# Both choices of three tiles summed on GpSimd, two tiles weighted there and scaled on ScalarE, in both tails of a two-layer hybrid step

## The reference

```python
def _rmsnorm(x, g):
    y = xf * rsqrt(mean(xf * xf, -1) + RMS_EPS) * g

for l in range(2):
    h = _rmsnorm(x, w['norm_mix'][l])
    mix = ...                      # l = 0: pool + mLSTM; l = 1: S5 + GLU
    x = x + mix
    x = x + _hmoe(_rmsnorm(x, w['norm_ffn'][l]), ...)   # each token: two experts, weighted
return _rmsnorm(x, w['norm_final']), states...
```

## Time and profile before

| what | us |
|---|---|
| median of 3 runs | 1101.48 (1100.95 to 1108.13) |
| span of the profiled execution | 1102.2 |
| TensorE busy | 951.2 (86%) |
| VectorE busy | 424.4 (39%) |
| GpSimd busy | 345.8 (31%) |
| ScalarE busy | 182.6 (17%) |

### The profile page before, as it was taken

One profiled execution on the slowest core, in us unless ns is written; L12 is line 12 of the kernel. 1 busy time (PEld: TensorE's weight loads), 2 busy tenths in 40 slices (PEclk: granted clock), 3 DMA queues, 4 the chain that ended last, 5 costly groups with the idle time before them and its releaser, 6 DMA issues.

```text
span 1102.2 us, 15831 instructions
## 1 busy us (share of the span) xinstructions
PE 951.2 (86%) x5716; PEld 576.6 (52%) x5716; DVE 424.4 (39%) x945; ACT 182.6 (17%) x353; POOL 345.8 (31%) x613
## 2 busy tenths in 40 slices
PE   3999989899888878787887379999989999787786
PEld 2788878555554444444445256444455555344442
DVE  5301155756652223223237971113465323221226
ACT  5311020222210000000034322102351000000003
POOL 1278900282266766656641000000020121101100
PEclk9999999899898999999998789999978999999998
DMA  7126850650679999999991964804046999999964
GB/s 255 39 77 225 302 236 3 251 181 33 266 282 391 425 419 421 408 405 409 401 346 69 102 83 171 363 5 168 19 165 274 419 421 425 424 423 424 424 271 189
DMA packets 53600, 292.39 MB, mean 265 GB/s; under 512 B 11633, under 2 KB 22001, under 8 KB 34071
## 3 DMA queue, kind: packets, MB, share of 16 engines
q1 hardware_dynamic: 41607, 270.29, 63.1%
q0 software_dynamic: 8640, 16.03, 3.9%
q10 hardware_dynamic: 3296, 5.31, 1.8%
HBM read 270.47 MB, written 36.80 MB: 279 GB/s over the span
## 4 chain that ended last, share of the span: by engine, by line
PE 54%; DMA 28%; DVE 6%; SPq 5%; issue 3%; POOL 2%; ACT 1%; POOLq 0%; DVEq 0%; ACTq 0%
DMA arena<-in_w_gu 16%; PE ps L734 13%; PE ps L858 10%; PE ps L1002 9%; PE ps L1197 5%; DMA arena<-in_w_down 4%; PE ps L992 3%; DMA arena<-scratch_hd,idx_now 2%; SPq L565 2%; DMA arena<-scratch_yd 2%; PE ps L929 2%; PE ps L1154 2%; DMA arena<-scratch_kp 2%; PE ps L1150 2%; PE ps L888 2%
## 5 line engine op out<-in xcount | busy, mean ns | idle before, releaser
L1002 PE MATMUL ps<-arena 128*64 128x256 f32 x2048 | 238.9, 389 | 52.6 <-DMA arena<-in_w_gu 52.6
L1002 PEld LDWEIGHTS ps<-arena 128*64 128x64 f32 x2048 | 148.4, 140 | 143.5 <-DMA arena<-in_w_gu 45.9
L2345 POOL TENSOR_TENSOR arena<-arena 128x256 f32<-128x256 f32 (+3 forms) x192 | 132.3, 689 | 41.7 <-POOL arena L2345 41.4
L734 PE MATMUL ps<-arena 128*128 128x260 f32 x640 | 141.7, 383 | 0.0
L2246 POOL TENSOR_TENSOR arena<-arena 128x32 f32<-128x32 f32 (+5 forms) x202 | 93.0, 461 | 155.1 <-DMA arena<-in_s_d 74.1
L992 PE MATMUL ps<-arena 128*64 128x512 f32 x512 | 125.1, 632 | 13.9 <-DMA arena<-in_w_down 13.3
L734 PEld LDWEIGHTS ps<-arena 128*128 128x128 f32 x640 | 121.1, 190 | 18.7 <-issue 0.4
L858 PE MATMUL ps<-arena 128*128 128x512 f32 x256 | 118.7, 616 | 3.9 <-DVE arena L1758 3.7
L1977 DVE TENSOR_TENSOR arena<-arena,ps 128x128 f32<-128x128 f32 x64 | 18.3, 288 | 255.7 <-ACT arena L1447 255.6
L1447 ACT ACTIVATE arena<-ps 128x128 f32<-128x128 f32 x64 | 17.7, 277 | 467.9 <-PE ps L1002 467.9
L1593 DVE TENSOR_TENSOR arena<-arena 128x32 f32<-128x32 f32 (+18 forms) x125 | 70.2, 561 | 36.1 <-DMA arena<-scratch_rows 22.2
(11 more groups left out here) (225 smaller groups left out, 971.6 us busy)
## 6 DMA issues: line engine op xcount, KB each, us to landing
arena<-in_w_gu SPq DMA_DIRECT2D x64, 2048.0 KB, 13.1
arena<-in_w_down SPq DMA_DIRECT2D x64, 1024.0 KB, 13.9
arena<-in_w_in SPq DMA_DIRECT2D x10, 1024.0 KB, 6.0
scratch_yd<-arena SPq DMA_DIRECT2D x2, 4160.0 KB, 18.7
arena<-scratch_yd SPq DMA_DIRECT2D x16, 512.0 KB, 7.9
arena<-in_w_out SPq DMA_DIRECT2D x1, 4096.0 KB, 12.1
scratch_hd<-arena ACTq DMA_DIRECT2D x8, 512.0 KB
arena<-in_w_glu SPq DMA_DIRECT2D x2, 2048.0 KB, 7.7
```

The lines of the kernel that those rows point to most:

```text
L734: mm = pe.matmul(o[:, b, 0:HALF], w[:, kc, (n % 2) * P:(n % 2 + 1) * P], HT[:, kc, b * HALF:(b + 1) * HALF], start=kc == 0, stop=kc == KC - 1)
L1002: mm = pe.matmul(ps[CAP * f:CAP * f + CAP, 2 + s, 0:256], XT[l][:, kc, CAP * s:CAP * s + CAP], WGU[l][i][s][:, kc, 256 * f:256 * f + 256], ...
L2345: g_.tensor_tensor(o, x, y, f).then_inc(sem("matrix_steps"), 1)
```

## The change

In both tails:

- GpSimd adds both choices of the last three tiles in order (k = 2, 3, 4) into the first one's place (`summed`). TensorE's `stored(k)` is dropped for these; its sum in PSUM is the last pair's rows alone. VectorE's `add_stored(k)` for k of 2 and more now waits for that sum (`choices_summed`) as well.
- GpSimd multiplies X of k = 0 and 1 by the norm's vector (`weighted`, into `WEIGHTED`), and ScalarE scales these rows by the reciprocal root (`scaled_rows`), k = 0 behind `tile_root(2)` and k = 1 behind the last root. VectorE scales only k = 2, 3, 4. In layer 0 ScalarE's first one also waits for `rows_added`, which VectorE gives after the last stored add and `add_last(3)`.
- VectorE's order is rewritten around that.
- Waits for `h_2` and `h_4` become waits for three tiles and for ScalarE's two; SP's final stores go in the order of tiles 0, 2, 3, 1, sample rows.
- The final norm's vector has a place of its own, `GBF`, and its load is issued between the waits for the two scatter counters, ahead of all loads of gathered rows.
- The semaphores of the first input loads and of the gathered rows are one family now (`tile_in_i`), with counts to match.

```diff
+        GBF = place(A + 21504, D)
+        WEIGHTED = [[place(A + at, D) for at in (8192, 9216)], [YG[1][t][1] for t in range(2)]]
...
                 sp.wait_ge(sem(f"y_out_{l}_1"), 112)
+                if l:
+                    load(GBF, T["norms"][4], "norm_in")
                 sp.wait_ge(sem(f"y_out_{l}_0"), 128)
-                for k, t in enumerate(combined_order(l)):
+                for t in combined_order(l):
                     for j in range(2):
                         at = NT * j + P * t
-                        load(YG[l][t][j][0:ROWS[t]], yd[l][at:at + ROWS[t]], f"yg_in_{t}")
-                    if l and k == 0:
-                        load(GB, T["norms"][4], "norm_in")
+                        load(YG[l][t][j][0:ROWS[t]], yd[l][at:at + ROWS[t]], f"tile_in_{t}")
...
-            for i in range(TILES):
-                sp.wait_ge(sem("h_4"), i + 1)
+            for i, (ready, n) in ((0, ("rows_by_act", 3)), (2, ("h_4", 1)), (3, ("h_4", 2)), (1, ("rows_by_act", 4))):
+                sp.wait_ge(sem(ready), n)
...
                         picked(0)
+                        stored(1)
                         for k in range(1, 5):
                             if k == 3 and l == 0:
                                 pe.wait_ge(sem("m_copied"), 17)
                             if k == 4:
                                 pe.wait_ge(sem(f"combined_{l}"), 1)
-                            stored(k)
                             picked(k)
...
+                def scaled_rows(k):
+
+                    t = combined_order(l)[k]
+                    act.wait_ge(sem("weighted_by_pool"), 2 * l + k + 1)
+                    act.wait_ge(sem("rstd_ready"), 2 * l + k + 1)
+                    if l == 0:
+                        act.wait_ge(sem("rows_added"), 1)
+                    out, src = norm_of_experts(l, t)[1], WEIGHTED[l][k]
+                    a.activation(out, src if l else by_group(src), ACT.Copy, scale=rstd[:, t:t + 1]
+                                 ).then_inc(sem("rows_by_act"), 1)
+
                 for k, t in enumerate(combined_order(l)):
                     act.wait_ge(sem(f"combined_{l}"), k + 1)
                     tile_squares(act, 2 * l + 2, t, JUNK[l], k)
                     tile_root(act, 2 * l + 2, t, k)
+                    if k == 2:
+                        scaled_rows(0)
+                scaled_rows(1)
                 if l == 0:
-                    act.wait_ge(sem("h_2"), 4)
+                    act.wait_ge(sem("h_2"), 2)
                     fill_pad(step)
...
-                        for k in range(3):
-                            add_stored(k)
+                        add_stored(0)
+                        add_stored(1)
                         add_last(0)
-                        add_stored(3)
+                        add_stored(2)
+                        variance(0)
                         add_last(1)
-                        variance(0)
-                        add_stored(4)
+                        for k in range(2):
+                            add_stored(k + 3)
+                            recip(k)
+                            dve.sem_inc(sem("rstd_ready"), 1)
+                            variance(k + 1)
+                            add_last(k + 2)
+                        dve.sem_inc(sem("rows_added"), 1)
+                        variance(3)
                         dve.wait_ge(sem("norm_in"), 8 * nn_ + 16)
-                        for k in range(5):
-                            if k < 3:
-                                add_last(k + 2)
-                            if k < 4:
-                                variance(k + 1)
+                        recip(2)
+                        add_last(4)
+                        scale(2)
+                        variance(4)
+                        for k in (3, 4):
+                            recip(k)
                             scale(k)
...
+                        def summed(k):
+                            t = order[k]
+                            m = ROWS[t]
+                            pool.wait_ge(sem(f"tile_in_{t}"), 32 * l + 48)
+                            one, other = (YG[l][t][j][0:m] for j in range(2))
+                            g_.tensor_tensor(one, one, other, ALU.add).then_inc(sem("choices_summed"), 1)
+
+                        def weighted(k):
+                            t = order[k]
+                            pool.wait_ge(sem("norm_in"), 16 * l + 32)
+                            pool.wait_ge(sem(f"combined_{l}"), k + 1)
+                            pool.wait_ge(sem(f"down_done_{l}"), E)
+                            g_.tensor_tensor(WEIGHTED[l][k], X[:, t, :], GBF if l else GB, ALU.mult
+                                             ).then_inc(sem("weighted_by_pool"), 1)
+
+                        summed(2)
+                        weighted(0)
+                        summed(3)
+                        summed(4)
+                        weighted(1)
```

More of the change, by code:

```diff
@@ L434, in norm_of_experts @@
             if l:
-                return X[:, t, :], HC[:, t, :], GB
+                return X[:, t, :], HC[:, t, :], GBF
             if t == TILES:
@@ L482, in _ @@
             for i in range(TILES):
[L483 removed]
+                load(X[:, i, :], every_fourth(T["x_prompt"], i), f"tile_in_{i}")
                 if i == 0:
@@ L587, in turns @@
                         sp.wait_ge(sem(f"combined_{l}"), r + 4)
-                        sp.wait_ge(sem(f"h_{2 * l + 2}"), 5)
+                        sp.wait_ge(sem(f"h_{2 * l + 2}"), 3)
+                        sp.wait_ge(sem("rows_by_act"), 2 * l + 2)
                         if l == 0:
@@ L1062, in picked @@
                             for b in range(2):
-                                mm = pe.matmul(last_slot(k)[0:m, b, :], PICK[l][:, t, 0:m], YL[l][:, b], start=False, stop=True)
+                                mm = pe.matmul(last_slot(k)[0:m, b, :], PICK[l][:, t, 0:m], YL[l][:, b], start=k >= 2,
+                                               stop=True)
                             mm.then_inc(sem("picks_by_pe"), 1)
@@ L1117, in _ @@
                                  for n in range(GU // 4)])
-            pe.wait_ge(sem("h_2"), 5)
+            pe.wait_ge(sem("h_2"), 3)
+            pe.wait_ge(sem("rows_by_act"), 2)
             rows_of_tiles = HX.rearrange("p g i c -> p (g i c)")
@@ L1278, in x_in @@
                     act.wait_ge(sem("cleared"), 1)
-                act.wait_ge(sem(f"x_in_{i}"), 16)
+                act.wait_ge(sem(f"tile_in_{i}"), 16)
             def ht_out(i):
@@ L2035, in add_stored @@
                             m = ROWS[t]
-                            dve.wait_ge(sem(f"yg_in_{t}"), 32 * l + 32)
+                            dve.wait_ge(sem(f"tile_in_{t}"), 32 * l + 48)
+                            if k >= 2:
+                                dve.wait_ge(sem("choices_summed"), 3 * l + k - 1)
                             step(v.tensor_tensor(X[0:m, t, :], X[0:m, t, :], YG[l][t][0][0:m], ALU.add))
@@ L2048, in variance, with recip @@
                             tile_variance(dve, nn_, order[k], k)
+                        def recip(k):
+                            tile_recip(dve, step, nn_, order[k], k)
                         def scale(k):
                             t = order[k]
-                            tile_recip(dve, step, nn_, t, k)
                             dve.wait_ge(sem(f"combined_{l}"), k + 1)
@@ L2099, in _ @@
             experts(0)
+            dve.wait_ge(sem("rows_by_act"), 2)
             step(v.memset(U[:, :, 0:NS], 0.0))
@@ L2435, in turns @@
                     if isinstance(r, int):
+                        order = combined_order(l)
+                        def summed(k):
[16 more added lines that the diff above has]
+                        weighted(1)
                         return most_rows
```

10 lines of the change are left out of this document (5 added, 5 removed).

## The result

The changed kernel takes 1118.03 us (median of 4 runs, 1115.29 to 1119.14) against 1102.52 for the kernel before beside it: ratio 1.012, 95% interval 1.0091 to 1.015. Timed again with five rounds (run e1) it takes 1116.77 against 1105.27 in 17 runs: 1.010 (1.0079 to 1.0121). So it is slower by about 1.1%, 11.5 to 15.5 us, where I had forecast 8.6 and a top of the range of 1114.5.

A forecast was written before the change was run, and what follows sets the result against it. Each tail was taken as bound first by landings, then by VectorE and ScalarE in turn. First tail 5.2, second 3.0 and stores 0.4 made 8.6 us on a median of 1101.5, forecast 1110 us, range 1103.5 to 1114.5.

The forecast's parts named there:

- the price of the product: GpSimd's multiplication of 1,024 columns by the norm's vector in both tails: 1.9 us, against 2.35 for an in-place sum.
- the stores: End of the second tail: tiles 3 and 1 issued together, 1 MB ahead of the last store, 0.4 us more.
- the norm vector: Loading the last norm vector ahead of layer 1's gathered rows: worth 0, bound 1.3 us sooner.
- the base: Starting time of the whole kernel, 1101.5 us, the median of the runs shown.
- the signs named: Expected in the changed profile, among others: VectorE idle some 3 us before each fourth stored add; first pad copy at 597 to 598.
- VectorE's add follows within 0.06 and holds GpSimd: Second tail, after GpSimd's first sum: VectorE's stored add (1.22 us) goes ahead of GpSimd's first product.
- case (d): TensorE's half clock around S5 comes sooner, lasts longer: up to 3 us; with 2.5 per GpSimd operation 1115. Chance 0.14.
- the replay of the old order: Second tail of the old kernel, replayed step by step: ends at 1100.1, its row at 1099.8; replays differ by 3.0.
- Rival (b): Layer 1's gathers: the lagging DMA engine is not the same, so the vector's move brings 1.3: 1108.8. Chance 0.17.
- tiles 1 to 3 land as before: Layer 1's gathers, vector moved early: tile 0 lands 1.3 later, the next three tiles unchanged, so worth 0.
- (a): No blocking between GpSimd and VectorE in the tails, which then cost 4.9 us: 1106.4. Chance 0.12.
- (c): GpSimd's tail work fits under the landings, kernel not slower; with 1.2 us per operation 1099.9 to 1101.2. Chance 0.05.

The follow-up runs named there:

- e4: Changed kernel, but GpSimd waits for VectorE's stored add before its first product, third sum and second product in each tail: 1116.09 us, ratio 1.0086 to the kernel before.
- e2: Kernel before with only the last norm vector's own buffer and early load, both tails as before: ratio 0.999 to the kernel before.
- e8: Changed kernel, ScalarE scaling its second tile before the sample's squares, rows stored in order 0, 2, 1, 3: ratio 1.0139 to the kernel before.
- e10: Changed kernel, ScalarE scaling its second tile before the sample's squares, rows stored in order 0, 1, 2, 3: 1113.55 us, run once for its trace.
- e9: Changed kernel plus eight counts of an unread semaphore on VectorE in each tail: 1115.73 us, run once for its trace.
- e7: Changed kernel with GpSimd's five operations of layer 1's tail on 16 of 1,024 columns, all waits kept: 1109.67 us, ratio 1.0043 to the kernel before.
- e6: Changed kernel with only GpSimd's three sums per tail; VectorE scales all five tiles in the old order: ratio 1.0076 to the kernel before.
- e5: Changed kernel with only GpSimd's two products per tail; TensorE adds all second choices again: ratio 1.0004 to the kernel before.
- e11: Changed kernel with the last norm vector loaded behind tile 0's two choices, into its own buffer: 1116.59 us, run once for its trace.

## Why the prediction missed

In short: that GpSimd's sums lengthen both tails was right. What failed is the order at each meeting of the two engines, the price of the product, the stores, the norm vector, the start of S5, which had no term, and the base.

**The direction and the places** were right: both tails longer, VectorE waiting for GpSimd in each, GpSimd's operations held to 3.3 us beside a stored add (forecast 3 to 3.6), ScalarE's squares late behind the scaled rows (1.28 of waiting at 1104.16), the second tail cheaper than the first. Of the signs named, one came out in another form: VectorE waits only 1.0 ahead of the fourth stored add, not some 3, and the rest lies inside the third, which takes 3.3. And the first pad copy came at 598.6, not at 597 to 598.

**Who comes first.** The step "VectorE's add follows within 0.06 and holds GpSimd" failed. It rested on 0.1 between GpSimd's operations; the trace has -0.04, and GpSimd is at work when the add starts 0.11 after the sum's end. e4, which makes the step true, gives its price: 0.9 us in each tail.

**The products' price.** I took 1.9 for a product, by the ratio of the 256- and 512-column rows, and 2.35 for a sum. Both take 2.35. The sums were hit exactly; the products were 0.45 short. The bound of 2.5 for all five was in the text, but only in case (d). In the prediction's steps only the first product of a tail lies on the path, and everything behind it moves by 0.45: with VectorE first that gives 5.65 and 3.45, where e4 measured 5.5 and 4.2. Order and price together are 0.9 + 0.9 + 0.9 = 2.7, and the tails missed by 1.1 + 2.1 = 3.2. Of the 0.75 that is left in tail two, 0.3 is the replay of the old order, which ended that much behind its row and was still taken off; the rest, and the 0.15 too much in tail one, I leave open. The estimate that the prediction worked out from the Trainium skill, GPSIMD Engine Reference, section on elementwise cycle accounting, 2.2 us for each kind, was nearer for the products than my ratio.

**The norm vector** was put at 0, its bound at -1.3. In the stretch ahead of tile 2 it gave 0.8 to 2; no comparison of whole times is clear of nothing. Rival (b) was right in kind. Half of the step held: in e2 tile 0's add came 1.0 later (forecast 1.3). The other half failed, "tiles 1 to 3 land as before": they came 1.4 to 2.3 sooner. It rested on taking the single engine at the end of the scatter for the one that is late at tile 3, from two busy shares that name no engine; no run shows which engines these were.

**The stores** were put at 0.4 and cost 1.3. I counted 1 MB ahead of the last store, and that was right: in the changed kernel tile 2's rows are through at 1109.0, and from 1109.2 to 1111.8 two full tiles move at 395 GB/s. Its price was wrong. That is one full tile more than in the kernel before (512 KB at the 420 GB/s of the earlier trace rows are 1.25 us), since tile 1 was held to the end by ScalarE's order and by SP's. e8 changed the first and the end came only 0.2 nearer (3.5); with the second as well, in e10, it took 2.6.

**The start of S5** had no term and cost 1.2 us. VectorE's gap between the clearings is 1.56 longer (1.73 against 0.17), which by e9 goes with the number of its instructions; its last scaling is 0.47 longer beside GpSimd's first start-state product, which the prediction had moving along "under work that moves by 5"; and 0.83 comes off, for which VectorE had waited for TensorE.

**The rivals.** (a), no blocking, is out by the adds of 3.28 to 3.33, which e4 brings back to 1.22. (c), GpSimd fits, is out by e7: full-size operations cost 7 us more than tiny ones. (d), the clock, would have given about the right time for a reason that isn't there:

```profile
586.40:600.00 13.60, 3.67 (x64) 3.10 (x64) 11.81 (x17) 7.64 (x14) 6.44 (x5) 0.50 0.29 96
600.00:603.40 3.40, 2.21 (x24) 1.93 (x24) 0.90 (x2) 2.02 (x4) 3.09 (x5) 1.00 0.01 2
603.40:610.20 6.80, 3.58 (x60) 3.40 (x64) 4.00 (x11) 2.20 (x6) 0.52 (x1) 0.50 0.02 4
```

(Busy by stretch, the changed kernel, columns as in the earlier trace rows.) The half level comes sooner and lasts longer, 20.4 us in two pieces instead of 10.2. But the first piece ends before S5's first products (600.76 us), which stood at half level before (594.28); they take 2.21 us now and took 3.82. Behind them nothing is added: VectorE's first copy is 7.7 us late, the driven products of S5 7.6 and SP's transfer behind those 7.2. The price named, a third of a stretch paid again, appears nowhere.

**The size of the whole.** With what the traces show, the sum of the terms would have been 8.6 + 1.8 (order) + 0.9 (products) + 0.5 (rest of the tails) + 1.2 (start of S5) + 0.9 (stores) - 2 (vector) = 11.9. The rest of the distance, from 1110 to 1117 or 1118, is the base: I set out from a median of three runs, 1101.5, and 17 runs have 1105.3. The range ended at 1114.5, while its own case (d) came to 1115.

## What to carry to other kernels

An operation given to an idle engine is priced by where its result is awaited: a sum on GpSimd between a landing and VectorE's add cost 2.3 us of latency and 2.1 more where the next operation held the add, though it took nothing from VectorE and relieved an engine that VectorE hardly waited for. Where two engines can't read SBUF at once, ask at each meeting which has its next instruction ready, for that one went first in each of these. Compare stretches between two fixed events before whole times: in the changed tails they repeat to 0.05 us, in the old first tail to 0.5, while whole runs spread over up to 9. And take the base from enough runs: here the median of three was 3.8 us off that of 17, half of the miss.

## What the runs showed of the hardware

Of two operations in a row on GpSimd, the second starts 0.04 us before the first one's end, and an operation of VectorE on two SBUF inputs that was waiting for the first comes 0.11 after it and is held for the whole of the second: 3.28 to 3.33 instead of 1.22, in each of the four places, and in every trace with this order. That a VectorE instruction with two SBUF inputs and a GpSimd instruction that reads SBUF lock each other out, and the one that starts first goes through whole, is stated by the Trainium skill, SBUF — State Buffer, section on the two separate sides; the traces agree, and add that between two GpSimd operations in a row there was no gap to start in.

An operation of 1,024 columns on two SBUF inputs takes GpSimd 2.33 to 2.37, product or in-place sum alike, though at 256 and 512 columns they differ by 0.09 and 0.21.

Where both start within 0.2 us of each other, the starts in the trace tell who was held. At VectorE's last scaling of the first tail GpSimd's first start-state product (256 columns) started 0.02 before to 0.05 after it in the changed kernel, e1, e4 and e6: VectorE was held, 1.69 to 1.75 instead of 1.28, and the product took 0.63. It started 0.09 to 0.21 after it in e5 and e7 to e11: VectorE took 1.28, and the product 1.56 to 1.67.

VectorE stood 1.7 us between two clearings, with a packet of instructions arriving 0.35 us into the first. Eight instructions more moved the gap ahead of both, where VectorE stood 3.1 in place of 0.9.
